# Norms of two VectorE instructions per chunk, chunkwise first tiles, and the first layer's modulation shared by TensorE and VectorE

## The reference

```
mod = silu(c) @ w_mod[l] + b_mod[l]          # 1024 -> 6 * 1024, for c and c_ctx
sh1, sc1, ga1, sh2, sc2, ga2 = split(mod, 6)
h = rmsnorm(x, g_norm1[l]) * (1 + sc1) + sh1
p = h @ w_in[l]                              # the first block mixes by Fourier, mLSTM, attention
x = x + ga1 * (mix(p) @ w_out[l])
x = x + ga2 * (square(relu((rmsnorm(x, g_norm2[l]) * (1 + sc2) + sh2) @ w_up[l])) @ w_down[l])
...
x = rmsnorm(x, g_final)                      # between the two blocks
# second block: the same frame, ada = silu(c_2) @ w_ada_2[l] + b_ada_2[l], 8 query heads over
# 2 key/value heads (GQA), dilated attention, gates
```

## Time and profile before

| | |
|---|---|
| median of 3 runs | 4170.23 us (4167.85 to 4176.98) |
| the profiled execution's own time | 4174.6 us |
| its span (first to last instruction) | 4172.8 us |
| PE busy | 3699.1 us (89%) |
| DVE busy | 2209.6 us (53%) |
| ACT busy | 1193.8 us (29%) |
| POOL busy | 294.8 us (7%) |
| mean granted TensorE clock | 0.931 |

### The profile page before, as it was taken

The page is one execution under the profiler, slowest core; times in us unless marked ns, Lnnn a source line. Parts: engine busy times, 40 slices in busy tenths (PEclk is TensorE's granted clock), DMA queues, the critical chain, the costliest instruction groups (busy, mean ns, idle before and its releaser), DMA issues.

```text
span 4172.8 us, 47186 instructions
## 1 busy us (share of the span) xinstructions
PE 3699.1 (89%) x17862; PEld 2922.7 (70%) x17862; DVE 2209.6 (53%) x3036; ACT 1193.8 (29%) x1473; POOL 294.8 (7%) x300
## 2 busy tenths in 40 slices
PE   7699788899999798888998789788999889788998
PEld 7576565688888575656886547676878547676787
DVE  7445533756566455337666635346666635344343
ACT  0224423312122234233222333222222333222322
POOL 0000000101000000001000100001110100001100
PEclk9999898899999898898999799898999899898999
DMA  7110110222322111104443101123443111122222
GB/s 269 71 61 31 41 50 12 92 94 100 111 91 81 67 51 51 60 15 152 161 151 111 57 34 70 41 91 133 159 162 131 67 35 68 41 91 81 91 91 101
DMA packets 51873, 361.52 MB, mean 87 GB/s; under 512 B 5904, under 2 KB 7568, under 8 KB 9616
## 3 DMA queue, kind: packets, MB, share of 16 engines
q1 hardware_dynamic: 36032, 259.01, 17.3%
q10 hardware_dynamic: 15696, 100.51, 6.6%
HBM read 357.40 MB, written 2.10 MB: 86 GB/s over the span
## 4 chain that ended last, share of the span: by engine, by line
PE 45%; issue 37%; DVE 12%; ACT 4%; POOL 1%; DMA 1%; ACTq 0%; POOLq 0%; DVEq 0%
PE pair L498 19%; PE pair L796 6%; PE pair L507 4%; PE pair L701 2%; PE pair L549 2%; PE pair L518 2%; PE pair L862 1%; DVE arena L1675 1%; PE pair L719 1%; DVE h_lo L1732 1%; DVE arena L1728 1%; PE pair L746 1%; DVE w_lo L1618 1%; PE pair L919 1%; PE pair L804 1%
## 5 line engine op out<-in xcount | busy, mean ns | idle before, releaser
L498 PE MATMUL pair<-h_hi,w_hi 128*128 128x512 f32 (+5 forms) x2176 | 762.7, 386 | 107.0 <-DVE h_lo L1732 62.5
L498 PE MATMUL pair<-h_hi,w_lo 128*128 128x512 f32 (+5 forms) x2176 | 748.2, 379 | 0.0
L498 PE MATMUL pair<-h_lo,w_hi 128*128 128x512 f32 (+5 forms) x2176 | 748.0, 379 | 0.0
L1618 DVE TENSOR_TENSOR w_lo<-raw,w_hi 128x2048 fp32r<-128x2048 f32 x229 | 525.0, 2293 | 348.7 <-ACT w_hi L1113 346.1
L1113 ACT ACTIVATE w_hi<-raw 128x2048 fp32r<-128x2048 f32 x229 | 436.5, 1906 | 807.5 <-PE pair L498 647.5
L498 PE MATMUL pair<-u_hi,w_hi 128*128 128x512 f32 (+1 forms) x1520 | 515.3, 375 | 65.7 <-DVE u_lo L1750 50.0
L498 PEld LDWEIGHTS pair<-h_hi,w_hi 128*128 128x128 f32 (+2 forms) x2176 | 386.7, 192 | 219.2 <-issue 94.4
L1634 DVE SCALAR_TENSOR_TENSOR x<-pair,mod,x 128x512 f32<-128x512 f32 (+1 forms) x408 | 274.3, 690 | 459.6 <-PE pair L498 458.9
L498 PE MATMUL pair<-u_lo,w_hi 128*128 128x512 f32 (+1 forms) x1520 | 509.3, 371 | 0.0
L498 PE MATMUL pair<-u_hi,w_lo 128*128 128x512 f32 (+1 forms) x1520 | 508.8, 371 | 0.0
L498 PEld LDWEIGHTS pair<-h_hi,w_lo 128*128 128x128 f32 (+2 forms) x2176 | 386.1, 191 | 81.0 <-issue 0.6
(11 more groups left out here) (265 smaller groups left out, 4343.6 us busy)
## 6 DMA issues: line engine op xcount, KB each, us to landing
raw<-in_wt_dram SPq DMA_DIRECT2D x230, 1024.0 KB, 4.8
arena<-in_modw_dram ACTq DMA_DIRECT2D x84, 1024.0 KB, 4.8
arena<-in_modw_dram SPq DMA_DIRECT2D x12, 1024.0 KB, 5.1
arena<-in_fconst_dram ACTq DMA_DIRECT2D x2, 2688.0 KB, 9.3
x<-in_xt_dram SPq DMA_DIRECT2D x1, 3072.0 KB, 10.5
arena<-in_brope_dram ACTq DMA_DIRECT2D x4, 640.0 KB, 4.0
out_dram<-x SPq DMA_DIRECT2D x1, 2048.0 KB, 7.2
arena<-in_headw_dram ACTq DMA_DIRECT2D x8, 208.0 KB, 2.4
```

What stands on the lines that cost most here:

```text
L498: mm = pe.matmul(pp[p][0:m, lo:hi], a[0:rows, k * width + c0:k * width + c0 + m], b[0:rows, k, lo:hi], start=(k == 0 and i == 0), stop=(k ...
L1618: dve.tensor_tensor(w_lo[slot][:], raw[slot][:], w_hi[slot][:].bitcast(F32), ALU.subtract)\
```

## The change

1. The modulation of layer 0 is split another way. Tiles 0 to 13 go by SP into three slots, and tiles 14 to 17 follow later. PE multiplies them with cact (2 columns) as the stationary operand and the tile as the moving one (mod_row: 8 products per tile, each 2 x 256). The row results are copied by ACT and turned back into columns on PE (turn). Tiles 18 to 23 go by ACT's queue and are folded on DVE. Only the first 12 tiles, which the first norm needs, are turned before it. Tiles 14 to 17 are multiplied after the norm's sum of squares (norm_mod), and their turning is in fourier.
2. ACT's squares and DVE's sums of x, and with them the load of x, stand between the folds instead of behind the stage. cv is the first DMA on ACT's queue, and x comes behind three modulation tiles on SP's.
3. In every norm the last square is not added by DVE; PE multiplies it by ones as well (twice the products). 
4. Per chunk DVE now has two instructions, each over two segments where n is 768: n_t = x * gain * n_r, and h_lo = (n_t + shift) - h_hi. POOL has none, and n_t has four buffers instead of two.
5. The first tile's two jobs both go chunk by chunk (first_jobs) in fourier, mlp_group and gqa.
6. In gqa three full tiles stand for five: keys with head pair 0, pairs 1 and 2, pair 3 with the values. Values and maxima stand elsewhere in the order.

The core of the diff:

```diff
-        n_t = [area((4 + i) * T_ALL, T_ALL) for i in range(2)]
-        n_f = [area((6 + i) * T_ALL, T_ALL) for i in range(2)]
+        n_t = [area((4 + i) * T_ALL, T_ALL) for i in range(4)]
...
+            def mod_tile(ti, slot):
+                sp.dma_start(mod_first[slot].rearrange("p a b -> p (a b)"), io["modw"][ti]).then_inc(mod_in[slot], 16)
+            for ti in range(MOD_EARLY):
+                if ti == 3:
+                    sp.dma_start(x[:].rearrange("p a b -> p (a b)"), io["xt"]).then_inc(x_in, 16)
+                if ti >= 3:
+                    sp.wait_ge(mod_used, MOD_FIRST + ti - 2)
+                mod_tile(ti, ti % 3)
             n_tiles = io["wt"].shape[0]
-            with t.loop(n_tiles // 2, "tiles") as i:
+            for slot in range(2):
+                sp.wait_ge(w_lo_done, t.next(w_lo_done))
+                sp.dma_start(raw[slot][:], io["wt"][slot]).then_inc(raw_in[slot], 16)
+            sp.wait_ge(mod_used, MOD_FIRST + 12)
+            mod_tile(14, 2)
+            sp.wait_ge(fold_done, MOD_FOLD - 1)
+            mod_tile(15, 3)
+            sp.wait_ge(fold_done, MOD_FOLD)
+            mod_tile(16, 4)
+            sp.wait_ge(mod_used, MOD_FIRST + 15)
+            mod_tile(17, 2)
...
+            def first_jobs(w, outs, n, signals):
+                for k in range(KC):
+                    h_wait(k)
+                    for c, out in enumerate(outs):
+                        for i, (a, b) in enumerate(passes(w, H)):
+                            for lo, hi in segments(n):
+                                mm = pe.matmul(out[:, lo:hi], a[:, k * 256 + c * P:k * 256 + (c + 1) * P], b[:, k, lo:hi],
+                                               start=(k == 0 and i == 0), stop=(k == KC - 1 and i == 2))
+                        if k == KC - 1:
+                            mm.then_inc(signals[c], 1)
...
+                for ti in range(MOD_EARLY):
+                    if ti % 4 == 0:
+                        take_pair((0, 1, 0, 2)[ti // 4])
+                    mod_row(ti, ti % 3, rows[ti // 4][0:2, ti % 4 * 256:(ti % 4 + 1) * 256])
+                    if ti in (5, 9):
+                        turn(ti // 4 - 1, rows_first, 8)
+                    if ti in (3, 5, 7, 9, 11, 13):
+                        folded((ti - 3) // 2)
+                turn(2, rows_first, 8)
...
+            def mod_row(ti, slot, out):
+                pe.wait_ge(mod_in[slot], t.next(mod_in[slot], 16))
+                for k in range(KC):
+                    mm = pe.matmul(out, cact[:, 0, k, :], mod_first[slot][:, k, :], start=(k == 0), stop=(k == KC - 1))
...
+                plain_job(0, [(pp[0][:, a:b], ones[:], n_acc[:, a:b], True, False) for a, b in segments(n)], None)
+                pe.wait_ge(last_sq, t.next(last_sq))
+                for a, b in segments(n):
+                    mm = pe.matmul(pp[0][:, a:b], ones[:], n_sq[1][:, a:b], start=False, stop=True)
+                mm.then_inc(job_act, 1)
+            def norm_mod():
+                take_pair(3)
+                for ti in range(14, 18):
+                    out = pp[2][0:2, ti % 4 * 256:(ti % 4 + 1) * 256] if ti < 16 else \
+                        pp[3][0:2, (ti - 16) * 256:(ti - 15) * 256]
+                    mod_row(ti, (2, 3, 4, 2)[ti - 14], out)
...
-                for c in range(2):
-                    feature_job(w, KC, P, c * P, P, 256, H, n, c, tile_used if c else job_act,
-                                None if c else h_wait)
+                take_pair(0)
+                take_pair(1)
+                first_jobs(w, (pp[0], pp[1]), n, (job_act, tile_used))
                 pair_read(0)
                 pair_read(1)
+                if n > S:
+                    turn(3, rows_first, 8)
+                    turn(4, rows_last, 4)
...
-                w = tile()
-                bank_product(w, 0, 256, 0, job_act, h_wait)
-                values(w, 0, 1, job_act)
+                take_pair(0)
+                take_pair(1)
+                first_jobs(tile(), (bank(0), bank(1)), S, (job_act, tile_used))
                 pe.wait_ge(const_in["gqa"], t.next("gqa", 16))
                 bank_rope(0, g_sq[0], g_qg[0])
+                w = tile()
+                bank_product(w, 0, 256, 0, job_act)
+                bank_rope(1, g_sq[1], g_qg[1])
+                bank_product(w, P, 256, 1, tile_used)
+                bank_rope(0, g_sq[0], g_qg[0])
+                t.next(rope_done)
+                maxima(0)
+                w = tile()
+                bank_product(w, 0, 256, 0, job_act)
+                bank_rope(1, g_sq[1], g_qg[1])
+                maxima(1)
+                values(w, 0, 1, job_act)
+                bank_rope(0, g_sq[0], g_qg[0])
                 values(w, 1, 0, tile_used)
-                bank_product(tile(), 0, P, 1, tile_used)
-                bank_product(tile(), 0, P, 0, tile_used)
-                t.next(rope_done)
-                for j in range(4):
-                    bank_rope(1 - j % 2, g_sq[(j + 1) % 2], g_qg[(j + 1) % 2])
-                    if j + 2 < 4:
-                        bank_product(tile(), 0, P, 1 - j % 2, tile_used)
-                    if j:
-                        maxima(j - 1)
+                maxima(2)
...
+                more(2)
+                square(0, T_ALL)
+                square(1, T_ALL)
+                rows(0, 0)
+                more(3)
+                square(2, T_ALL)
+                square(3, T_ALL)
+                rows(1, 1)
+                square(4, T_ALL)
+                square(5, T_ALL)
+                more(4)
+                square(6, T_ALL)
+                square(7, T_ALL)
+                more(5)
+                rows(2, 0)
...
+                first_fold(0)
+                dve.wait_ge(x_in, 16)
+                dve.sem_inc(x_done, KC)
+                first_fold(1)
+                for j in range(4):
+                    add_square(j, T_ALL)
+                first_fold(2)
+                first_fold(3)
+                for j in range(4, KC):
+                    add_square(j, T_ALL)
+                first_fold(4)
+                first_fold(5)
...
-                    finish(dve.tensor_tensor(n_t[j % 2][:, 0:n], x[:, j, 0:n], n_r[:, 0:n], ALU.mult), dve_act)
+                    if j >= 4:
+                        dve.wait_ge(h_ready, t.now(h_ready) - (KC - j + 3))
+                    for s, (a, b) in enumerate(segments(n)):
+                        ins = dve.scalar_tensor_tensor(n_t[j % 4][:, a:b], x[:, j, a:b], gain[:, which, j, s:s + 1],
+                                                       n_r[:, a:b], ALU.mult, ALU.mult)
+                    ins.then_inc(dve_act, 1)
+                def low(j):
+                    heard()
+                    for s, (a, b) in enumerate(segments(n)):
+                        ins = dve.scalar_tensor_tensor(h_lo[:, j, a:b], n_t[j % 4][:, a:b],
+                                                       mod[:, 24 * which + j, s:s + 1], H32[:, j, a:b],
+                                                       ALU.add, ALU.subtract)
+                    ins.then_inc(h_ready, 1)
+                t.next(h_ready, KC)
+                scaled(0)
                 scaled(1)
                 for j in range(KC):
-                    if j % 2 == 0:
-                        dve.wait_ge(t_even, t.next(t_even))
-                        if j:
-                            scaled(j + 1)
-                    for s, (a, b) in enumerate(segments(n)):
-                        ins = dve.tensor_scalar(n_f[j % 2][:, a:b], n_t[j % 2][:, a:b], gain[:, which, j, s:s + 1],
-                                                mod[:, 24 * which + j, s:s + 1], ALU.mult, ALU.add)
-                    finish(ins)
-                    heard()
-                    dve.tensor_tensor(h_lo[:, j, 0:n], n_f[j % 2][:, 0:n], H32[:, j, 0:n], ALU.subtract)\
-                       .then_inc(h_ready, 1)
+                    low(j)
+                    if j + 2 < KC:
+                        scaled(j + 2)
...
-        tiles.append(_w_tile(w[:, 512:768]))
-        for j in range(4):
-            tiles.append(_w_tile(np.concatenate([w[:, 64 * b:64 * b + 64] for b in (j, j + 4)], 1)))
+        heads = [np.concatenate([w[:, 64 * b:64 * b + 64] for b in (j, j + 4)], 1) for j in range(4)]
+        keys, values = w[:, 512:640], w[:, 640:768]
+        for pair in ((keys, heads[0]), (heads[1], heads[2]), (heads[3], values)):
+            tiles.append(_w_tile(np.concatenate(pair, 1)))
```

227 lines of the change are left out of this document (126 added, 101 removed).

## The result

The changed kernel takes 4067.85 us (median of three undisturbed executions, 4066.86 to 4072.62; with a fourth, disturbed one of 6471.93 the median is 4070.23), the kernel before 4170.8 in the same comparison: ratio 0.9754, 95% interval 0.9735 to 0.9773. Run again later as `e10_changed_again` it took 4073.34 (4064.47 to 4076.25), ratio 0.9765 (0.975 to 0.978). The forecast was 4070.

What follows compares the result with a forecast made beforehand. PE was taken to pace the first stage, DVE or PE the later norms. Terms -57, -5, -7, -10, -6.5, -5, -9 and +1 sum to -98.5 from 4174.6: 4076, by the median 4072, said as 4070; range 4042 to 4090, widened to 4125.

Steps and rivals of the forecast that it cites:

- What bounds the kernel: PE, not transfers, paces the first modulation; in the MLPs' first groups DVE leads in layers 0 to 2, PE in layer 3.
- the price of a row tile: First modulation: eight products of a row tile cost 3.88 us at PE's high clock level, with bounds 3.88 and 7.7.
- B: Rival: row tiles run at PE's low clock level, 7.7 us each, 4145 (chance 0.1); mixed case 4108 (chance 0.15).
- D: Rival: each row tile costs over 9.3 us, loads and drain not hidden, so the kernel is slower; chance 0.03.
- C: Rival: transfers bind the first stage, 24 MB at 247 GB/s, +16 us, 4087; chance 0.1.
- The stage, -57: Start to Fourier's first product: first norm at 85 instead of 144, Fourier's products at 129 instead of 186.25, -57 us.
- gqa, -5 and -9: New order laid out by hand, 82.5 us from 88.4: -5 in layer 3; -9 in layer 2, where slow values should vanish.
- values with rope 12.3: Step of the hand layout of gqa's new order: the values with their rope take 12.3 us.
- Norms elsewhere: Norms after the first: 2.1 us per chunk at 768 columns, 1.4 at 512; last h_lo -6.6 and -4.6 us.
- Where DVE leads: Second norm of layers 0, 1, 2: the group shifts with the last h_lo, -5 in layer 0, -7 in layers 1 and 2.
- The doubled sum: Sum of squares multiplied twice by PE in each norm: net +1.7 us at 768 columns, +1.2 at 512.
- Rival E: Later norms' gains fail as PE's doubled job falls to the low level between chunks, 4085 to 4095; chance 0.07.

Runs made afterwards that it cites:

- e10_changed_again: The changed kernel run again without an edit: 4073.34 us, ratio 0.9765 to the kernel before.
- Experiment 4: Changed kernel with gqa's order and tiles as before the change, norms and first stage as changed: 4054.71 us, ratio 0.9721.
- Experiment 5: Changed kernel with a chunk's norm steps as before (three instructions, POOL scaling the even chunks), everything else as changed: 4111.34 us, ratio 0.9841.
- experiment 7: Changed kernel with gqa's values moved into PE's pauses and the last square added by DVE again, with one sum over partitions: 4027.54 us, ratio 0.9641.

## Why the prediction was right, and where it was not

*What bounds the kernel* and *the price of a row tile* were right. PE sets the stage's pace; row tiles run at the high level; B and D fall with 3.53 us per tile, C with a stage in which PE waited for no transfer (up to 1.12 us in the profiles of the experiments), though DMA at 99% shows that it was nearer than I thought. The Trainium skill ("TensorE: Matmul & The Clock Gate", What's actually happening) was the ground for expecting full speed from a busy PE; this stage agrees (jobs at 0.35 from 96.75 on), the stage before doesn't: PE was busy without a break from 30 to 126, and at 124.14 its eight products by ones still took 1.84 us, where they take 1.05 between row tiles. The forecast gave another reason, a pass of 0.64 at 173, and that one proves nothing, since PE had been idle for 18.05 us in between the earlier trace rows. The profile's column of the granted clock says 1.00 at both places, so the level there is read from durations alone.

*The stage, -57:* the mechanism held, each size in it was too careful, and all to the same side. Tiles, sums, turns and slow start took 60.3 us from PE's start to its end at 74.9 instead of 67, with PE's start at 14.56 instead of 15 and 3.1 behind its end as laid: the norm's sum at 77.95 instead of 85. Doubled sum 4.4 instead of 5.8, late tiles 13.9 instead of 15.5, jobs 16.9 instead of 19 (no slow start behind row tiles), copies and turns 1.8 instead of 4. Together 14 us; in the second profile PE started at 17.41, and it was 12.

*gqa, -5 and -9:* the step that failed is the layout by hand. In layer 3 its jobs (from the first chunk's start), copy and rope, products and maxima came out as laid (15.9, 2.6, 22.7 and 28.2 us against 15.5, 3.1, 21.6 and 30), but "values with rope 12.3" took 18.9: it gave them the high level because jobs stream ahead, and the order puts them behind a wait of 3.33. And it never laid out the old order in the new norm. Experiment 4 does: without the order -8.2 and -13.5, order +8.0 and +6.0. The order, forecast at -1.6 and -5.6, is a loss, and the norm's part was underrated, by 4.8 and 10.1. "Two tiles less cost nothing" may stand; it isn't what decides.

*Norms elsewhere:* DVE's 2.1 and 1.4 per chunk were right, the reason given was not. "DVE's own work does not shrink" adds up instructions of 0.86 and 0.96, but before, one in every two chunks was stretched beside POOL's product (2.37 instead of 0.86 at 768 columns, 1.65 instead of 0.69 at 512), so DVE's time did shrink, and its waits in between were only some 0.16 us per two chunks. Experiment 5 puts the change of steps at 32 to 41 us over the kernel, where the terms of the forecast make 37. In layer 1's first norm it takes 19.3 us from the first chunk's start to the end of the jobs (1302.95 to 1322.27), where it took 33.8 and 21.2 were forecast. *Where DVE leads:* PE's wait for u_lo ends 7.0, 4.9 and 5.4 us sooner behind Exp in layers 0, 1 and 2, forecast 6.6, 4.6 and 4.6. The wait itself grew from 3.88 to 5.12 in layer 0, a little more than the 1 us allowed, and one of 3.74 for w_lo came ahead of it; the first pass behind them takes 1.01, low level. *The doubled sum* costs 0.9 us in layer 3's first norm and 8.5 over nine norms (experiment 7), near the +1.2 to +1.7 per norm taken.

*Rival E* was true in part: the doubled jobs start at the low level (0.43 per pass of 512, then 0.23), 13.46 us instead of 11, 2.5 in this norm. This stands behind the wait of 3.95 us for the first chunk; waits between chunks, which E blamed, there are none.

So the forecast had 12 to 14 us too little in the stage, 6 too much in gqa, and the rest in stretches that vary by 6 to 9 us between executions: that 4070 was met so closely is luck, in that these cancel. The terms given for its range (-6, -7, -8 and +15) make 4049 to 4085, not the 4042 to 4090 stated; the result lies in both.

## What to carry to other kernels

When a new order is laid out by hand, the old order must be laid out under the other changes too, or a loss by the order hides in a gain by the rest. What stood behind a wait here cost up to double (10.43 instead of 5.31), so the work to place in a wait is that which would otherwise come right after it: the same instructions in another order gave 34 us. Durations of an engine's instructions are to be read in place, not by their shape alone: beside another engine's product the same one took 1.66 instead of 0.69. And with two accumulators, work of another engine that is longer than a job moves a wait rather than filling one.
